# A one-core Trainium2 transformer kernel: an RMS sum, a rescaling, a table step and a reload change their places in a hand-written order

## The reference

```python
# first block, layer 0 (x and ctx each): adaLN on rms_norm, gMLP gating + Fourier mixing
h = rms_norm(x, norm_g[0]) * (1 + scale) + shift
x = x + gate * mixer_ab(h);  ctx = ctx + gate_c * mixer_ab(hc)
# layer 1: windowed attention with sink, 16 heads
x = x + gate * ((attention(h) * silu(g)) @ w_out_c)
x = rms_norm(x, final_g)                      # end of the first block
# second block: forgetting attention + 31-tap depthwise causal convolution, then SwiGLU
h = rms_norm(x, mix_pre_g) * (1 + sc1) + sh1
y = concat([fox_attention(h), silu(layer_norm(conv(...)))]) @ w_o
x = x + g1 * rms_norm(y, mix_post_g)
h = rms_norm(x, ffn_pre_g) * (1 + sc2) + sh2
y = (silu(h @ Wg) * (h @ Wu)) @ w_ffn_out     # 2816 hidden channels
return x + g2 * rms_norm(y, ffn_post_g)
```

## Time and profile before

| | |
|---|---|
| three runs, median (lowest to highest) | 2339.71 us (2337.65 to 2339.76) |
| the profiled execution | 2339.76 us, of which 2338.0 us from the first to the last instruction |
| PE / DVE / POOL / ACT busy | 95% / 68% / 66% / 37% of the span |
| granted clock of PE, mean | 0.984 |
| DMA | 314 MB, mean 134 GB/s |

### The profile page before, as it was taken

The page is one execution under the profiler, slowest core; times in us unless marked ns, Lnnn a source line. Parts: engine busy times, 40 slices in busy tenths (PEclk is TensorE's granted clock), DMA queues, the critical chain, the costliest instruction groups (busy, mean ns, idle before and its releaser), DMA issues. The chain is left out here.

```text
span 2338.0 us, 32528 instructions
## 1 busy us (share of the span) xinstructions
PE 2227.6 (95%) x11183; PEld 1859.4 (80%) x11183; DVE 1589.2 (68%) x2296; ACT 855.1 (37%) x1538; POOL 1531.4 (66%) x1401
## 2 busy tenths in 40 slices
PE   5999999999999999999998988999999999999998
PEld 3788889788888877777876867777788888888887
DVE  4854656668795699986889979877887344444434
ACT  3321112223221688863343337844321222222213
POOL 2755556745994788746789943457788766666652
PEclk9999999999999999999998999999999999999999
DMA  9345445514467556534343476553443211111152
GB/s 368 109 127 169 130 142 164 181 50 154 145 189 235 161 159 172 137 113 166 87 131 96 149 186 162 158 178 106 158 135 90 73 55 54 55 55 54 53 182 90
DMA packets 197729, 314.33 MB, mean 134 GB/s; under 512 B 34044, under 2 KB 86968, under 8 KB 196288
## 3 DMA queue, kind: packets, MB, share of 16 engines
q1 hardware_dynamic: 161520, 221.43, 33.1%
q10 hardware_dynamic: 36048, 90.82, 10.4%
HBM read 251.34 MB, written 60.85 MB: 134 GB/s over the span
## 5 line engine op out<-in xcount | busy, mean ns | idle before, releaser
L1405 PE MATMUL PS<-HXH,WH 128*128 128x512 f32 x1664 | 660.3, 397 | 33.0 <-DVE HXL L2866 5.6
L1406 PE MATMUL PS<-HXL,WH 128*128 128x512 f32 x1664 | 652.6, 392 | 0.0
L1407 PE MATMUL PS<-HXH,WL 128*128 128x512 f32 x1664 | 652.3, 392 | 0.0
L1233 POOL TENSOR_SCALAR WH<-RAW 128x512 fp32r<-128x512 f32 x400 | 317.9, 795 | 423.7 <-PE PS L1407 289.2
L1236 POOL TENSOR_TENSOR WL<-RAW,WH 128x512 fp32r<-128x512 f32 x400 | 570.1, 1425 | 33.4
L1405 PEld LDWEIGHTS PS<-HXH,WH 128*128 128x128 f32 x1664 | 315.4, 190 | 107.1 <-POOL WL L1236 5.7
L1406 PEld LDWEIGHTS PS<-HXL,WH 128*128 128x128 f32 x1664 | 315.7, 190 | 66.2 <-issue 1.9
L1407 PEld LDWEIGHTS PS<-HXH,WL 128*128 128x128 f32 x1664 | 315.1, 189 | 66.8
L3166 DVE TENSOR_TENSOR Y<-PS,Y 128x1024 f32<-128x1024 f32 x56 | 68.4, 1224 | 101.0 <-PE PS L1407 101.0
L1382 POOL TENSOR_SCALAR PB<-PB,RC 128x640 f32<-128x640 f32 (+1 forms) x128 | 98.7, 779 | 51.5 <-DVE RC L3383 51.4
L1405 PE MATMUL PS<-AHH,WH 128*128 128x512 f32 x320 | 124.9, 390 | 0.8 <-ACT Y L2393 0.4
(11 more groups left out here) (413 smaller groups left out, 4813.1 us busy)
## 6 DMA issues: line engine op xcount, KB each, us to landing
RAW<-in_ada_w SPq DMA_DIRECT2D x160, 256.0 KB, 2.8
RAW<-in_w_in_ab SPq DMA_DIRECT2D x88, 256.0 KB, 2.7
XX<-XR ACTq DMA_DIRECT2D x4, 4096.0 KB, 14.2
RAW<-in_w_in SPq DMA_DIRECT2D x56, 256.0 KB, 2.6
RAW<-in_w_ffn_in SPq DMA_DIRECT2D x112, 128.0 KB, 2.2
RAW<-in_w_ffn_out SPq DMA_DIRECT2D x54, 256.0 KB, 3.4
XR<-XX ACTq DMA_DIRECT2D x3, 4096.0 KB, 13.4
RAW<-in_w_in_c SPq DMA_DIRECT2D x40, 256.0 KB, 2.6
```

Source lines behind the costliest of these rows:

```text
L1233: g.tensor_scalar(WH[:, sw, 0:m], raw_of(n)[:, 0:m], 1.0, 0.0, ALU.mult, ALU.add).then_inc(gpsimd_done, 1)
L1405: mm(out, wh, xh, start=first, stop=False, **kw)
L1406: mm(out, wh, xl, start=False, stop=False, **kw)
L1407: return mm(out, wl, xh, start=False, stop=last, **kw)
```

## The change

Four places of the order are rearranged.

1. `sum` of `h1` in the first norm moves ahead of the `stat` of `h0`; the `stat` of `h1` becomes an event of its own after the `apply` of `h0` instead of a `mid` of `("u", "h0")`; the `stat` of `c` takes that place, and `apply` of `c` comes before the `adav` event and the product `("xb", "h1")`. `turn=True` falls away. The `c` part uses the common buffers `SUM` and `RST`.
2. `xw` of `h0` moves from the `wo` stage to the front of the convolution stage; there the order `conv -3`, `xw h1`, `flogz` becomes `xw h0`, `xw h1`, `flogz`, `conv -3`. The spill of `h0` follows its `xw`, and the `xw` no longer waits for reload 2. `R1` gets another address.
3. The third `tk` event moves from between the two output products of `ch` 0 to ahead of the first. The order of the products stays.
4. Reload 3 becomes an event behind `pages`, and in it the two tables are issued before x.

```diff
+    ev("sum", ("sum", 0, "h1"), n=0, part="h1")
     ev("stat", ("stat", 0, "h0"), n=0, part="h0")
...
     ev("apply", ("apply", 0, "h0"), n=0, part="h0")
-    ev("sum", ("sum", 0, "h1"), n=0, part="h1")
+    ev("stat", ("stat", 0, "h1"), n=0, part="h1")
...
-    lin(("xb", "h0"), "ab", "xb", "h0", w, last=True, turn=True)
+    lin(("xb", "h0"), "ab", "xb", "h0", w, last=True)
     ev("small", "small")
-    ev("statpost", ("statpost", 0, "h1"), n=0, part="h1")
     ev("apply", ("apply", 0, "h1"), n=0, part="h1")
+    ev("statpost", ("statpost", 0, "c"), n=0, part="c")
...
-    lin(("u", "h0"), "ab", "u", "h0", w, last=True, mid=("stat", 0, "h1"), midk=2)
+    lin(("u", "h0"), "ab", "u", "h0", w, last=True, mid=("stat", 0, "c"), midk=6)
+    ev("apply", ("apply", 0, "c"), n=0, part="c")
...
+            for x in x2:
+                ev("xw", ("xw", x), part=x)
+            ev("flogz", "flogz")
             ev("conv", ("conv", -3), i=-3)
-            ev("xw", ("xw", "h1"), part="h1")
-            ev("flogz", "flogz")
...
-        if (g, p) == (1, "h0"):
-            ev("xw", ("xw", "h0"), part="h0")
...
+    ev("tk", ("tk", 2), k=2)
     for ch in range(2):
-        w = out_weights(ch)
-        hidden_out(ch, "h1", w, gs=(0,))
-        if ch == 0:
-            ev("tk", ("tk", 2), k=2)
-        hidden_out(ch, "h1", w, gs=(1,))
+        hidden_out(ch, "h1", out_weights(ch))
...
     ev("pages", "pages", blocks=blocks, outs=outs)
+    ev("reload", ("reload", 3), n=3)
...
+                    else:
+                        act.wait_ge(b12_stored, upto("b12out"))
+                        act.wait_ge(products_done, upto("P", PAGES - 1, 4))
+                        for x, (hl, k0) in enumerate(((HXH, 0), (HXL, 4))):
+                            act.dma_start(hl[:, k0:k0 + 4, HALF:T].bitcast(F32), B12D[x]).then_inc(b12_loaded, 16)
                     act.dma_start(XX[:, :, :], XR).then_inc(x_loaded, 16)
```

More of the change, by code:

```diff
@@ L157, in plan @@
     w = weights("ab", "xb")
-    lin(("xb", "h0"), "ab", "xb", "h0", w, last=True, turn=True)
+    lin(("xb", "h0"), "ab", "xb", "h0", w, last=True)
     ev("small", "small")
-    ev("statpost", ("statpost", 0, "h1"), n=0, part="h1")
     ev("apply", ("apply", 0, "h1"), n=0, part="h1")
+    ev("statpost", ("statpost", 0, "c"), n=0, part="c")
     w = weights("ab", "u")
-    lin(("u", "h0"), "ab", "u", "h0", w, last=True, mid=("stat", 0, "h1"), midk=2)
+    lin(("u", "h0"), "ab", "u", "h0", w, last=True, mid=("stat", 0, "c"), midk=6)
+    ev("apply", ("apply", 0, "c"), n=0, part="c")
     w = weights("ab", "xb")
     adav(2, 0)
-    ev("statpost", ("statpost", 0, "c"), n=0, part="c")
-    lin(("xb", "h1"), "ab", "xb", "h1", w, last=True, mid=("stat", 0, "c"))
-    ev("apply", ("apply", 0, "c"), n=0, part="c")
+    lin(("xb", "h1"), "ab", "xb", "h1", w, last=True)
     w = weights("ab", "u")
@@ L506, in program @@
         RST0 = {p: at(f"RST0{p}", [HALF], F32, MREG + 8192 + 12288 * i) for i, p in enumerate(("h0", "h1"))}
+        RST0["c"] = RST
         PC = small("PC", [384])
@@ L518, in program @@
         EX = o[0]
-        SUM0C, RST0["c"] = at("SUM0C", [HALF], F32, EX + 4096), at("RST0c", [HALF], F32, EX + 6144)
         T1, T2 = ([at(f"T{i}{x}", [4, HALF], F32R, XREG + 16384 * i - 16384 + 8192 * j) for j, x in enumerate("HL")] for i in (1, 2))
@@ L581, in program @@
         RST2 = {p: at(f"RST2{p}", [HALF], F32, HREG + 73728 + 2048 * i) for i, p in enumerate(("h0", "h1"))}
-        R1 = {p: at(f"R1{p}", [HALF], F32, EX + 2048 * i) for i, p in enumerate(("h0", "h1"))}
+        R1 = {p: at(f"R1{p}", [HALF], F32, HREG + 77824 + 2048 * i) for i, p in enumerate(("h0", "h1"))}
         OUTS = [at(f"OUTS{b}", [2048], F32, HREG + 8192 * b) for b in range(2)]
@@ L717, in sum_of @@
         def sum_of(n, part):
-            return SUM2[part] if n == 2 else SUM3 if n == 3 else SUM1 if (n, part) == (0, "h1") else SUM0C if (n, part) == (0, "c") else SUM
+            return SUM2[part] if n == 2 else SUM3 if n == 3 else SUM1 if (n, part) == (0, "h1") else SUM
         def rstd_of(n, part, w=HALF):
@@ L2130, in _ @@
                     else:
-                        act.wait_ge(vector_done, upto("X", 2, "h0", 7) if (n, part) == (2, "h0") else upto("XW", n, part) if n == 2 else upto("X", 4, "h1", 7) if n == 3 else upto("XW", n))
+                        act.wait_ge(vector_done, upto("XW", n, part) if n == 2 else upto("X", 4, "h1", 7) if n == 3 else upto("XW", n))
                     if n == 0:
@@ L2154, in _ @@
                         act.wait_ge(vector_done, upto("H", "hload", 2, "h1", 7))
+                    else:
[3 more added lines that the diff above has]
+                            act.dma_start(hl[:, k0:k0 + 4, HALF:T].bitcast(F32), B12D[x]).then_inc(b12_loaded, 16)
+                            did(b12_loaded, "b12in", by=16)
                     act.dma_start(XX[:, :, :], XR).then_inc(x_loaded, 16)
@@ L2211, in _ @@
                                 did(scalar_done, ("sg", pg))
[L2212 to L2220, removed]
                             if i == 6:
@@ L2884, in _ @@
                     dve.wait_ge(vector_done, upto("r1", part))
-                    if part == "h0":
-                        dve.wait_ge(x_loaded, upto("reload", 2))
                     for k in range(KT):
```

## The result

The changed kernel takes 2369.53 us (median of 4 runs, 2367.07 to 2372.79) beside 2339.74 us for the kernel before on the same chip (4 runs): a ratio of 1.0128, 95% interval 1.0108 to 1.0146, which is +29.9 us (25.3 to 34.2). The prediction was 2367.9 us. The profiled execution took 2369.22 us, with a span of 2367.4 us against 2338.0.

What follows compares the result with a forecast made beforehand. PE, busy 2227.6 of 2338.0 us, was taken as the bound, edits priced by its holes. The four terms, -0.2 + 4.7 + 7.2 + 16.4 = +28.1 us on 2339.76, gave 2367.9 us, range 2354 to 2380 us.

Steps and rivals of the forecast that it cites:

- What bounds the kernel: Whole kernel: PE busy 2227.6 of 2338.0 us, holes about 110 us; an edit is worth what it does to a hole.
- Edit 1: First norm: first product at 54.3 instead of 52.00, low clock regained at `u h0`; -0.2 us, bounds -3.5 and +3.
- the gain at `u h0`: First norm: `u h0` starts 0.85 us later after a 1.5 us wait, not 2.93, so 1.6 us of low clock return.
- The 1.0 us for a short wait at `u h1`: First norm: `adav` ends later behind `apply c`, delaying weights; 1.0 us added, bounds 0 and 3.
- Edit 2: Convolution stage: `xw h0` makes DVE 8.2 us late at the fourth bank of `q2 h0`; +4.7 us, range 2.2 to 10.2.
- The next hole: PE's 3.35 us hole at 1270.85 shrinks to 1.25, giving back 2.1 us, and its 1.4 us of low clock.
- Edit 3: `tk` step: PE waits 5.6 us for ACT's first output copy, old 0.43 us gone; +7.2 us with clock, bounds 5.2 and 8.0.
- Edit 4: Reload: x lands at 2264.6, 19 us after issue begins; hole 14.4 us, +16.4 us with the clock.
- The low end: Reload: x overtakes the tables, landing at 2259.6; hole 9.4 us plus 1.4 us of clock.
- rival about the reload: Two: reload hidden, costing nothing, 2351.5 us, chance 0.04; reload jam or lasting low clock, above 2380 us, chance 0.06.
- the moved additions are cheap: Rescaling at or below zero, multiplications 0.75 us, attention holes swallow the rest, first norm gives 3: about 2360 us, chance 0.12.
- The front pays: Front: `u h0` right behind `small`, first product earlier; at most 12.1 us gained, total about 2337 to 2344 us, chance 0.04.

Runs made afterwards that it cites:

- x first: Kernel before with only the reload moved behind the pages, x issued ahead of the two tables: ratio 1.0034 (1.0020 to 1.0047), +8.0 us.
- edit 3 alone: Kernel before with only the third `tk` event moved ahead of the first `ch` 0 output product: ratio 1.0038 (1.0024 to 1.0052), +8.9 us.

## Why the prediction was right, and where it was not

- **What bounds the kernel** held: PE's idle times (25.2 us) and its longer busy time (4.2 us) make up the whole of the difference.
- **Edit 1** was forecast at -0.2 us, bounds -3.5 and +3, and measured +3.7 (1.6 to 6.1), +2.9 by the traces. The step that failed is that the first `adac` on DVE "frees the PSUM set of the second `adac` on PE", which "starts at about 46.8". I followed DVE's lateness to the job that waits for DVE and did not ask who waits for ACT's root itself. It is the job before, the second `ada` product, 5.34 us long in the kernel before, 6.58 here, and not begun before 43. The first product came 6.7 us late, not 2.3. The exchange of two PE jobs, which takes that wait away, brings it to 52.70.
- In the same sum the gain at `u h0` was priced on one execution. The wait there shrank to 1.58 us (forecast 1.5), and the stretch of lower clock behind it is gone. But in the seven other profiles with this front the wait is 1.58 to 2.58 us without any change (2.2 on the mean of the eight), and three of them, with 1.58, 1.58 and 1.68 us, have no lower clock there either. So 2.93 us and the full 1.6 us of clock were this execution's, and some 0.6 and 1.0 us were there to be won. The 1.0 us for a short wait at `u h1` didn't come either, though POOL's idle time behind `adav` grew from 14.19 to 16.34 us.
- **Edit 2**, +4.7 forecast, +5.1 measured. DVE was to be 8.2 us late at the fourth bank, and that bank came 10.3 us later (1255.66 against 1245.36), 0.3 of it from the front. The rescaling took 16.8 us, not 15.4, and two of the gate steps 1.05 and 2.08 us instead of 0.68 and 1.41. The next hole gave back 2.4 us (3.35 to 0.95; 2.1 forecast) and the lower clock behind it is gone, but over the whole stretch PE's busy time is the same within 0.2 us, so on balance no clock was won. By 1403 6.4 us were left, and in the attention 0.4 us more came back (1.3 against the mean of all). So the lateness was under-sized by some 2 us, and the trace has this edit at 5 to 6 us; the nearness of 4.7 to 5.1 is in part luck.
- The Trainium skill (SBUF — State Buffer, Who interferes with whom) says that a DVE instruction with two SBUF inputs and a GpSimd (POOL) instruction that reads SBUF block each other. The multiplications agree in direction: 0.75 us each with POOL idle, 1.22 beside its weight splits and 1.68 beside its adds. I had used it only for one length per instruction (1.5 us), and not for what the reordering does to it.
- **Edit 3**, +7.2 forecast (5.2 to 8.0): the wait was 5.82 us (5.6 forecast), the clock behind it 1.7 (2.0). +6.6 in the changed kernel and +9.0 alone by the trace (1.6 of it not the edit's, 2.2 of clock), +8.9 (5.6 to 12.2) by the time.
- **Edit 4**, +16.4 forecast, +15.6 by the trace, +17.5 (14.0 to 21.3) alone. The hole was 13.70 us (14.4): x landed 18.4 us after the first of the three was issued, and I had taken 19. The clock was 1.95 (2.0). The low end, in which x overtakes the tables, does not occur in this order: it is what x first shows, 7.75 + 2.8 (forecast 9.4 + 1.4). Neither rival about the reload came: it was not hidden and met no jam.
- **The sum** of 28.1 us came within 2 us of 29.9 because the edits that carry it (3 and 4, 23.6 us) were each a single wait with a known releaser. The miss of 3 us at the front is larger than the gap; by the traces edit 3 and edit 4 were forecast 0.6 and 0.8 us too high, which takes part of it back. That the total is nearer than its worst term is luck.
- Of the rivals, "the moved additions are cheap" was half true in a way that doesn't help: they are cheaper beside POOL's splits (1.22 us) and idle times (0.75), and the changed order puts the first eight beside its adds. "The front pays" was wrong in sign.

## What to carry to other kernels

When work is put ahead of an instruction, look for whoever waits for that very instruction before you follow the engine behind it: here it was the next user of a PSUM set, one job nearer than the one I priced. When work trades places, look at what runs beside it in the new place: here the taps kept their length and the rescalings did not. A late transfer is priced by its whole queue from the first issue, and both its place and its order count only once the slack is used up. And one profile's landmark is no baseline for a few microseconds: take the same stretch from several kernels in which it is unchanged, which a set of experiments on single edits contains anyway.

## What the runs showed of the hardware that was not expected

- The same instructions up to the product at 1084 ended anywhere between 1077.95 and 1083.86 in eight profiles. From the first product on the slowest of them needs 1031.9 us with PE busy for 992.9, that of edit 3 alone 1026.7 with 991.5: of the 5.2 us, 3.7 are idle time (2.93 against 1.58 at `u h0` is part of it) and 1.5 longer busy time. The stretch from the first gate row to the product behind the transposes, in which PE neither waits long nor loses clock, took 60.38 to 60.43 us in all eleven.
- Eight DVE multiplications with two SBUF inputs took 9.74 us in this stage beside POOL's weight splits, 13.42 beside its adds of block 3, and 11.70 to 12.05 beside some of each. Sixteen taps with one input in PSUM took 10.6 us beside the adds, and 10.6 us where splits and single adds ran beside them. A hole that is filled on one engine can be lost again in the length of its instructions.
- What was lost to the lower clock behind a wait did not grow with the wait: 1.7 us (changed kernel) and 2.2 (edit 3) behind 5.82 us, 2.8 (x first) behind 7.75, 1.95 (changed kernel) and 2.2 (edit 4) behind 13.7.
- The stretch from 1828 to 2233 took 404.7 us at a mean granted clock of 1.00 in five of the fourteen profiles, and 1.6 us more at 0.996 in the other nine, whatever the edit.
